# Turning two blocks of a cached page per instruction, and reordering the recurrence beside it

## The reference

```python
s_past = (einsum('blhr,bpr->bhlp', q_abs, ckv_past) + einsum('blhd,bpd->bhlp', q_pe, kpe_past)) * ATTN_SCALE
p      = softmax(concat([s_past, s_new]))
o_lat  = einsum('bhlp,bpr->blhr', p[..., :P], ckv_past) + einsum('bhlm,bmr->blhr', p[..., P:], ckv)
```

```python
sa = einsum('bhvk,bhk->bhv', S, kk_t)
S  = S * d_t[:, :, None, :] - sa[..., None] * b_t[:, :, None, :] + v_t[..., None] * k_t[:, :, None, :]
o  = einsum('bhvk,bhk->bhv', S, r_t)
```

## Time and profile before

| | |
|---|---|
| median of three runs | 2040.96 us |
| the profiled execution | 2037.07 us |
| its span, first to last instruction | 2035.4 us |
| TensorE busy (matmuls) | 1865.2 us, 92% |
| weight loads busy | 1164.3 us, 57% |
| VectorE busy | 895.6 us, 44% |
| ScalarE busy | 494.7 us, 24% |
| granted TensorE clock, mean | 0.970 |

### The profile page before, as it was taken

One profiled execution on the slowest core, in us unless ns is written; L12 is line 12 of the kernel. 1 busy time (PEld: TensorE's weight loads), 2 busy tenths in 40 slices (PEclk: granted clock), 3 DMA queues, 4 the chain that ended last, 5 costly groups with the idle time before them and its releaser, 6 DMA issues. The chain is left out here.

```text
span 2035.4 us, 45818 instructions
## 1 busy us (share of the span) xinstructions
PE 1865.2 (92%) x19360; PEld 1164.3 (57%) x19360; DVE 895.6 (44%) x1984; ACT 494.7 (24%) x1164; POOL 172.6 (8%) x158
## 2 busy tenths in 40 slices
PE   4899999999987999899949999999999879998898
PEld 2565676666654666654326656766666546665543
DVE  2024134222766676654230340332318577775542
ACT  3111012222412333311131110222224123333201
POOL 0010000011334000000000100000212240000000
PEclk9899999999999999979989999999999899999899
DMA  9500000000205666341075001010001166562411
GB/s 388 207 11 27 21 21 32 21 21 13 59 26 159 185 188 180 109 178 42 32 301 213 0 27 32 11 32 22 21 22 50 28 186 186 176 186 83 178 42 42
DMA packets 103927, 191.18 MB, mean 94 GB/s; under 512 B 17162, under 2 KB 87260, under 8 KB 100004
## 3 DMA queue, kind: packets, MB, share of 16 engines
q1 hardware_dynamic: 103716, 188.19, 27.9%
HBM read 175.41 MB, written 21.19 MB: 97 GB/s over the span
## 5 line engine op out<-in xcount | busy, mean ns | idle before, releaser
L771 PE MATMUL PB<-RB,R 128*128 128x344 f32 x1632 | 496.1, 457 | 0.0
L771 PEld LDWEIGHTS PB<-RB,R 128*128 128x128 f32 x1632 | 303.7, 191 | 159.6 <-issue 19.7
L1946 PE MATMUL PB<-RB,R 128*128 128x512 f32 x512 | 221.2, 593 | 0.0
L1589 PE MATMUL PB<-WUQ,Q 32*32 32x256 f32 x5120 | 191.0, 385 | 14.7 <-DVE WUQ L1748 9.4
L1748 DVE STREAM_TRANSPOSE WUQ<-RB 128x512 f32<-128x512 f32 x316 | 197.0, 676 | 5.5 <-DMA RB<-in_cache 5.3
L1946 PEld LDWEIGHTS PB<-RB,R 128*128 128x128 f32 x512 | 97.0, 190 | 120.8 <-issue 118.6
L931 ACT ACTIVATE R<-PB 128x344 f32<-128x344 f32 x90 | 41.2, 457 | 423.4 <-PE PB L771 423.4
L1184 DVE TENSOR_TENSOR PB<-PB,CST 128x128 f32<-128x128 f32 x64 | 18.8, 294 | 226.3 <-PE PB L791 226.3
L1589 PEld LDWEIGHTS PB<-WUQ,Q 32*32 32x32 f32 x5120 | 90.0, 104 | 46.0 <-DVE WUQ L1748 23.1
L619 PE MATMUL PB<-RB,R 128*128 128x344 f32 x288 | 88.5, 472 | 10.8 <-PEq L225 10.8
L619 PEld LDWEIGHTS PB<-RB,R 128*128 128x128 f32 x288 | 57.1, 199 | 41.4 <-issue 14.8
(11 more groups left out here) (355 smaller groups left out, 2619.6 us busy)
## 6 DMA issues: line engine op xcount, KB each, us to landing
RB<-in_cache SPq DMA_DIRECT2D x512, 160.0 KB, 2.6
R<-in_w_ada SPq DMA_DIRECT2D x16, 1536.0 KB, 17.4
R<-in_w_in SPq DMA_DIRECT2D x44, 512.0 KB, 3.7
RB<-in_w_out SPq DMA_DIRECT2D x8, 1024.0 KB, 9.9
RB<-out_x_stream SPq DMA_DIRECT2D x2, 4096.0 KB
out_x_stream<-RB SPq DMA_DIRECT2D x16, 512.0 KB
RB<-in_x_prompt SPq DMA_DIRECT2D x1, 4096.0 KB
RB<-in_w_kv SPq DMA_DIRECT2D x2, 1280.0 KB, 5.6
```

The costliest lines, as they stand in the source:

```text
L771: mm = pe.matmul(jobbank(j)[:, 0:CH], ring[:, blkno[n] % 4, k, :], hT[:, k, chunk(c)], start=(k == 0), stop=(k == KT - 1))
L1589: mm = pe.matmul(PB[qp[o], 2 * (h % 2) + q % 2, 0:256], Q4[qp[q], g, :], k[qp[q], c], start=(g == 0), stop=(g == NB - 1), skip_group_check ...
L1946: mm = pe.matmul(PB[0:n, 2 * (t % 2) + hf, :], mixT[:, k, cols(t)], wo[:, k, hf * 512:(hf + 1) * 512], start=(k == 0), stop=(k == 5))
```

## The change

Three edits. (1) A turn takes two blocks, 64 of the 320 columns, in one instruction of 128 x 1024 elements, into two neighbouring slots. kt_done and kt_used count pairs. At the place of an even S VectorE turns the next pair; TensorE waits before an even S and counts after an odd one. The turn in the stage before is merged likewise. (2) TA goes to bank 4, which it shares with PT, and waits for the copy of the probabilities of the even half instead of AK; PT of an odd half and Z wait for TA's copies; TB waits for AK. In STEPS Y5 and TB change places, so that an odd half ends with Y5, MX, TB, EX. (3) EX comes last in a half; an even half ends with Y2, MX, U1, X3, EX.

```diff
--- before.py
+++ after.py
@@ -1320,9 +1320,8 @@
                             dve.wait_ge(pg_in[0], 128)
                             dve.wait_ge(pg_in[1], 128)
                             pages = RB[:, HB[0]:HB[0] + 2 * QW].rearrange("p (s c) -> p s c", c=KW)
-                            for rb in range(2):
-                                dve.transpose(WUQ[:, rb * 512:(rb + 1) * 512].rearrange("p (j c) -> p j c", j=16),
-                                              pages[:, :, RP + 32 * rb:RP + 32 * rb + 32]).then_inc(kt_done, 1)
+                            dve.transpose(WUQ[:, 0:1024].rearrange("p (n j c) -> p j n c", n=2, j=16),
+                                          pages[:, :, RP:RP + 64].rearrange("p j (n c) -> p j n c", n=2)).then_inc(kt_done, 1)
 
 
             s_gs = sem("s_gs")
@@ -1402,7 +1401,7 @@
             fcol = lambda rb: RP + 32 * rb if rb < 8 else 32 * (rb - 8)
 
             STEPS = ["MA", "Z0", "X1", "U0", "Y1", "H0", "X2", "Z1", "Y2", "U1", "X3", "H1", "Y3", "OO",
-                     "X4", "AK", "Y4", "TA", "X5", "TB", "Y5"]
+                     "X4", "AK", "Y4", "TA", "X5", "Y5", "TB"]
             chain = ("Z", "U", "H", "O")
 
 
@@ -1418,7 +1417,7 @@
                     if rb < 8:
                         plan += [(h // 2, *mine.pop(0)), (h // 2, *mine.pop(0))]
                 rest = [(h // 2, *x) for x in mine]
-                plan += rest[:1] + [(h, "MX", 0)] + rest[1:2] + [(h, "EX", 0)] + rest[2:]
+                plan += rest[:1] + [(h, "MX", 0)] + rest[1:] + [(h, "EX", 0)]
             plan += [(NH - 1, "PT", 0), (NS, "rw", "Z0"), (NH - 1, "PV", 0), (0, "FC", 1), (NS, "rw", "U0"), (0, "FC", 2), (NS, "rw", "H0"),
                      (0, "FC", 3), (NS, "rw", "Z1"), (0, "FC", 4), (NS, "rw", "U1"), (0, "FC", 5), (NS, "rw", "H1"), (0, "FC", 6),
                      (NS, "rw", "OO")]
@@ -1475,14 +1474,14 @@
                                                start=True, stop=True, skip_group_check=True)
                             mm.then_inc(ak_full, 1)
                         elif n == "TA":
-                            pe.wait_ge(ak_done, p + 1)
+                            pe.wait_ge(pp_done, 2 * p + 1)
                             for f in range(2):
-                                pe.transpose(PB[:, 6, f * P:(f + 1) * P], A2[:, f, p * P:(p + 1) * P], ident)
+                                pe.transpose(PB[:, 4, f * P:(f + 1) * P], A2[:, f, p * P:(p + 1) * P], ident)
                             for f in range(2):
-                                mm = pe.transpose(PB[:, 6, (2 + f) * P:(3 + f) * P], pT[:, 2 + f, p * P + 1:(p + 1) * P + 1], ident)
+                                mm = pe.transpose(PB[:, 4, (2 + f) * P:(3 + f) * P], pT[:, 2 + f, p * P + 1:(p + 1) * P + 1], ident)
                             mm.then_inc(ta_full, 1)
                         elif n == "TB":
-                            pe.wait_ge(ta_done, p + 1)
+                            pe.wait_ge(ak_done, p + 1)
                             for f in range(2):
                                 mm = pe.transpose(PB[:, 6, f * P:(f + 1) * P], pT[:, 4 + f, p * P + 1:(p + 1) * P + 1], ident)
                             mm.then_inc(tb_full, 1)
@@ -1531,6 +1530,7 @@
                         i = 2 * p + c
                         bt, kt, vt = TOK[k][:, 0], TOK[k][:, 1], TOK[k][:, 2]
                         if n[0] == "Z":
+                            pe.wait_ge(ta_done, p + 1)
                             pe.wait_ge(tb_done, p + 1)
                             pe.wait_ge(st_done, i + 1)
                             for f in range(2):
@@ -1581,19 +1581,23 @@
                                 pe.wait_ge(sv_done, 1)
                             if g == 0 and h >= 2:
                                 pe.wait_ge(xe_done, h - 1)
-                            pe.wait_ge(kt_done, NB * h + g + 1)
+                            if g % 2 == 0:
+                                pe.wait_ge(kt_done, 5 * h + g // 2 + 1)
                             k = KTr[:, (NB * h + g) % 4].rearrange("p (s c) t -> p c s t", c=2)
                             for c in range(2):
                                 for q in (0, 2, 1, 3):
                                     o = 2 * (q // 2) + c
                                     mm = pe.matmul(PB[qp[o], 2 * (h % 2) + q % 2, 0:256], Q4[qp[q], g, :], k[qp[q], c], start=(g == 0), stop=(g == NB - 1),
                                                    skip_group_check=True, tile_position=(32 * q, 32 * o))
-                            mm.then_inc(kt_used, 1)
+                            if g % 2 == 1:
+                                mm.then_inc(kt_used, 1)
                         elif what == "PT":
 
                             pe.wait_ge(xe_done, h + 1)
                             if h:
                                 pe.wait_ge(pp_done, h)
+                            if h % 2 == 1:
+                                pe.wait_ge(ta_done, h // 2 + 1)
                             for s in range(4):
                                 mm = pe.transpose(PB[:, 4, s * P:(s + 1) * P], prb[:, s * P:(s + 1) * P], ident)
                             mm.then_inc(pp_full, 1)
@@ -1643,7 +1647,7 @@
                             op.then_inc(lo_done, 1)
                         elif n == "TA":
                             act.wait_ge(ta_full, p + 1)
-                            t6 = PB[:, 6, :].rearrange("p (v f w k) -> p v f w k", v=2, f=2, w=2)
+                            t6 = PB[:, 4, :].rearrange("p (v f w k) -> p v f w k", v=2, f=2, w=2)
                             for c in range(2):
                                 for w in range(2):
                                     op = act.activation(TOK[k][hp[w], 0:2, 2 * c:2 * c + 2, :], t6[hp[c], :, :, w, :], ACT.Identity)
@@ -1737,16 +1741,17 @@
                 @block.vector
                 def _(dve):
 
-                    def turn(n):
-                        h, rb = n // NB, n % NB
-                        if n >= 4:
-                            dve.wait_ge(kt_used, n - 3)
+                    def turn(i):
+                        h, rb = i // 5, 2 * (i % 5)
+                        if i >= 2:
+                            dve.wait_ge(kt_used, i - 1)
                         if rb == 0:
                             for q in (2 * h, 2 * h + 1):
                                 dve.wait_ge(pg_in[q % QS], 128 * (q // QS + 1))
                         pages = RB[:, HB[h % 3]:HB[h % 3] + 2 * QW].rearrange("p (s c) -> p s c", c=KW)
-                        op = dve.transpose(KTr[:, n % 4], pages[:, :, fcol(rb):fcol(rb) + 32])
-                        op.then_inc(kt_done, 1)
+                        o = 2 * (i % 2)
+                        dve.transpose(KTr[:, o:o + 2].rearrange("p n j c -> p j n c"),
+                                      pages[:, :, fcol(rb):fcol(rb) + 64].rearrange("p j (n c) -> p j n c", n=2)).then_inc(kt_done, 1)
 
                     dve.memset(S0[:, 0], 0.0)
                     dve.memset(Sg, 0.0)
@@ -1801,10 +1806,10 @@
                         elif what == "rw":
                             prepare(h, g)
                         elif what == "S":
-                            if NB * h + g + 2 < NB * NH:
-                                turn(NB * h + g + 2)
+                            if g % 2 == 0 and 5 * h + g // 2 + 1 < 5 * NH:
+                                turn(5 * h + g // 2 + 1)
                         elif what == "MX":
-                            dve.wait_ge(kt_used, NB * (h + 1))
+                            dve.wait_ge(kt_used, 5 * (h + 1))
                             dve.tensor_reduce(mxa, sc_(h), AX.XY, ALU.max)
                             dve.drain()
                             dve.tensor_copy(mxb[0:64], mxa[64:128])
```

## The result

The changed kernel took 2049.26 us (median of 6, 2042.84 to 2051.64), the kernel before on the same chips 2042.26 (6 runs, 2038.87 to 2044.92): ratio 1.0036 [1.002, 1.0051], slower by about 7.4 us. The forecast was +7.4, with a range of 2036 to 2056.

The account below looks back on a forecast made before the run. Neither engine is full; the wait that ends last at each place of a token's cycle bounds the kernel. 0.41 us over 16 cycles, plus 0.8 at the ends, gave +7.4 us, median 2048.4, range 2036 to 2056.

Parts of the forecast that it names:

- D: Length of one merged turn of two blocks on VectorE: 1.15 us, against 1.27 for a pair of single turns.
- Step 1: S4 and S5, even half: both blocks come at the merged turn's end, so PV starts 0.32 us later.
- Step 2: S8 and S9, even half: S8 0.49 us later; Y2 behind S9, the maxima and next turn also 0.49 later.
- rival B: Losses and gains cancel because VectorE keeps its saving from two pairs: 0 to +2 us, 2042, chance 0.26.
- Step 3: S2 and S3, odd half: S2 waits for the merged turn and starts 0.37 us later.
- the exponential's move: Exponential after X3's copy, freeing Y3: counted as nothing, hidden by the merged turn; about 0.4 us a cycle without the merge.
- Step 4: S8 and S9, odd half: nothing lost, since what follows waits for ScalarE in any case.
- TA, TB and Y5: Bank edit and new order at the odd half's end: +0.04 us a cycle, bounds -0.2 to +0.28.
- Sum: The cycle's loss of 0.41 us, 6.6 us over 16 cycles, plus 0.8 at the ends: +7.4 us.
- the end of a layer: Last PT of the decode stage waits for the exponential behind TB's copies: 0.4 us a layer, 0.8 in all.
- A: VectorE sets the pace and shorter turns pay: -5.8 us over 16 cycles, +0.8 at the ends, 2036, chance 0.21.
- C: The merged turn runs below the single one's rate or as two: near 1.34 us, total 2057, chance 0.09.

Follow-up runs that it names:

- n1: The kernel before with page loads from the seventh group of 8 pages on cut to one partition: 2033.42 us, 0.995.
- n3: The kernel before with the exponential last in a half and the later page loads cut to one partition: 2028.81 us, 0.9928.
- n2: The changed kernel with the later page loads cut to one partition: 2041.02 us, 0.9989 against the kernel before with full loads.
- e1: The kernel before with the merged turn alone; banks, order of steps and exponentials as before: 2050.26 us, 1.0032.
- e5: The kernel before with single turns, but TensorE starts a pair of blocks only when both are turned: 2050.42 us, 1.0038.
- e11: The changed kernel with blocks 4, 5 and 8, 9 of even halves turned and released singly again: 2038.9 us, 0.9993 against the kernel before.
- e8: The kernel before with block 4 of the even half turned ahead of MA's VectorE work: 2038.42 us, 0.9984.
- e2: The kernel before with only the exponential moved last in a half: 2041.45 us, 0.9994.
- e9: The kernel before with TA in bank 4, Y5 before TB, and X5's copy ahead of TA's on ScalarE: 2036.56 us, 0.9983.
- e10: The kernel before with the edits of e2, e8 and e9, plus blocks 8 and 9 of odd halves turned ahead of AK: 2035.93 us, 0.9973.

## Why the prediction was right

**D, the merged turn.** Forecast 1.15, measured 1.203. The straight line through 128 and 512 columns was too flat: 512 columns more cost 1.203 - 0.669 = 0.53 us, not 0.48. By the prediction's own steps that is 0.15 a cycle more, 2.4 us, and a forecast of +9.8. The estimate from "VectorE: DVE Perf Modes" of the Trainium skill (Specifications, 0.96 GHz), 1.20, was the right one; the trace agrees.

**Step 1 (S4 and S5, even half).** Forecast PV 0.32 late, measured 0.37 in the clean cycles and in after; with D = 1.20 the same step gives 0.37. One wait of 0.90, none at S5.

**Step 2 (S8 and S9, even half).** Forecast 0.49 for X3's side of the cycle; measured 0.60 at X3, and D = 1.20 accounts for it: the turn starts 0.05 later and lasts 0.05 longer. That VectorE then waits for Y2 (0.42 at 730.08) is what the step claimed against rival B.

**Step 3 (S2 and S3, odd half).** Forecast 0.37 at S2, with the exponential's move hidden; with D = 1.20 the same step gives 0.52, and 0.52 was measured, with a wait of 0.33 for the turn. The sum then carried this on to PT as it stood, and that was wrong: from S2 to PT it is 1.11 in the earlier trace rows and in n1, and 1.03 behind a wait, so 0.08 came back and PT is 0.44 late. That the exponential's move is worth 0.4 a cycle alone holds for a cycle without stops (n3: 0.5 in its shortest). Of the 6 to 7 us it brought 4.6 where the page loads are cut and 1.2 with them, at most 3.7 by the interval. The figure described the cycle, not the kernel.

**Step 4.** No loss at S8 and S9 of the odd half: the two MA differ by less (0.29) than the two PT (0.44).

**TA, TB and Y5.** The mis-sized term. Forecast +0.04, bounds -0.2 to +0.28; from PT to MA the clean cycles give 0.29 - 0.44 = -0.15. The order was as said (Y5 waits 0.76 for X5's copy, then TB, then S0), but Y5 came 2.60 after TA (743.67 less 741.07) in place of the 2.66 that I kept, and MA 1.78 after Y5 (745.45 less 743.67) in place of my 1.91: the change of tile shape that I counted between Y5 and TB, 0.17, is mostly not there.

**Sum.** 0.29 a cycle, 16 cycles: 4.6 us; at the end of a layer PT of n2 is 30.40 behind the last MA where n1's is 29.82, which is 0.58, of which 0.3 lies beyond the cycle's own: 0.6 in all, where I had 0.8. Together 5.2. The stages as a whole bear this out only when the stops of the last section are set aside: from the first MA to the last PT of both layers n2 takes 3.8 us more than n1 (476.1, 472.4), and 5.2 more with the mid-run stops taken off. Not every cycle is a clean one; the first two of a layer, for one, are together 0.4 to 0.7 shorter in n2. The rest of the 6.7 by which n2's profiled span is longer (2039.4, 2032.7) lies outside the stages, most of it in the stretch between them, where almost all of the code is the same; that stretch varies from 772.1 to 776.1 us over the 14 traces, so a single trace can't tell 2 us there.

So the forecast of +7.4 met the ratio partly by luck. The turn's true length would have made it 9.8; the 0.08 between S2 and PT, the order of Y5 (-0.15 where I had +0.04) and the end of the stage took about 4.5 of that back. The mechanism and the places are those forecast; 2 us between the steps' 5.2 and the measured 7.4 (7.6 in n2) stay open.

**The rivals.** A (VectorE sets the pace): fell with e1 and e5. The rule behind it, of the Trainium skill ("VectorE: DVE Perf Modes", on the fixed extra latency), that one large tile pays the latency once, agrees with VectorE's rows by about 0.07 us a pair (1.27 against 1.20), and the saving bought nothing where TensorE waited. B (they cancel): VectorE does wait for Y2, so its savings don't reach S2. C (D near 1.34): D is 1.203.

## What to carry to other kernels

Before two producer instructions are merged, look at who waits for the first one: the merge saves a fixed part (here about 0.07 us) and delays the first half by the whole second (here 0.53), and this costs wherever the consumer is that close. Leaving the two awaited pairs single took the loss away (e11: 1.0036 went to 0.9993); merging the pairs that were ready early did no harm and brought no gain that could be told. Moving the awaited turn ahead of other work did bring something (e8, 0.9984). And a wait that was taken off a cycle is not yet time: measure the edit alone, and if the gain is missing look for gaps without a releaser. A sum that comes out right is no proof of its terms: here four were off and three of them offset the first.

## What the runs showed of the hardware

TensorE's instructions themselves ran late. In the midst of 32 alike weight loads, with no wait written between them, the stream stops. The place is S0 and S1 of an odd half, in before (a whole row in 0.83, no stop) and in e2 (19 loads, a stop, 13 loads); weight loads of before, then of e2:

```profile
728.62 0.83 PEld L1589 LDWEIGHTS PB<-WUQ,Q 32*32 32x32 f32 x32
```

```profile
729.67 0.57 PEld L1589 LDWEIGHTS PB<-WUQ,Q 32*32 32x32 f32 x19
730.57 0.17 PEld L1589 LDWEIGHTS PB<-WUQ,Q 32*32 32x32 f32 x13 [0.33 <-issue]
731.15 0.20 PEld L1556 LDWEIGHTS PB<-R 64*64 64x64 f32 x4 [0.41 <-issue]
...
731.76 0.34 PEld L1522 LDWEIGHTS PB<-RB 32*32 32x32 f32 x32
```

The last row is Y3, which no longer waits for ScalarE: the stop took 0.33 of what that saved. In after the stop at the same place is 0.51 (732.14, shown above). Such stops lie 127 or 128 weight loads apart or multiples of that (in after behind the 1224th and 1352nd load of the first layer's stage, the 4658th and 4786th). With a matmul for each load that is about 256 instructions. The page of before, part 3, has a queue of instruction packets:

```profile
q8 instruction: 154, 2.52, 0.5%
```

2.52 MB in 154 packets is 16 KB a packet; if they were all TensorE's 38,720 instructions it would be 65 bytes each, so a packet would hold about 250. I read the stops as TensorE waiting for its next packet.

The kept traces have the start and the length of each packet of q8, and they settle that much. In the decode stages of all 14 traces there are 241 stops longer than 0.26 us between two weight loads of one line without a releaser. Every one of them ends 1.21 to 1.63 us after the end of a packet of q8, while these packets come 4.1 to 4.5 us apart in the median, and only about one weight load in ten of before's first stage lies in that stretch behind a packet. The packet took a median of 1.06 and 0.96 us in before's two stages.

Both layers' stages, from the first MA to the last PT, and these stops (gaps of 0.26 or less, most of them at PV and alike in every kernel, are not counted), in us:

| | stages | stops | stages less stops |
|---|---|---|---|
| before | 476.2 | 7.2 | 469.0 |
| after | 486.6 | 8.2 | 478.4 |
| e2 | 482.2 | 14.0 | 468.2 |
| e8 | 479.3 | 16.8 | 462.5 |
| e9 | 478.7 | 15.7 | 463.0 |
| e10 | 475.2 | 23.4 | 451.8 |
| n1 | 472.4 | 2.1 | 470.3 |
| n2 | 476.1 | 0.6 | 475.5 |
| n3 | 469.6 | 6.3 | 463.3 |

Where the kernel was made quicker the stops grew. With them set aside e10's stages are 17 us shorter than before's (24 were expected by the steps), e8's and e9's 6 (9 and 8), and n3's 7 shorter than n1's (5 to 7); only e2's, 1 us, stay far from their 6 to 7. The profiled execution of before was itself 4 to 5 us under the medians of its kernel, so these differences are low if anything. That is where most of e10's missing gain went, as far as single traces can tell. With the page loads cut the stops shrink from 7.2 to 2.1, which is 5 of the 10.2 us by which n1 is quicker.

What stays open: why the page loads make the stops longer, since the packets themselves took no less time without them (1.12 and 1.15 us in n1); why a quicker cycle stops more; and stops between unlike instructions, which are not in this count and may be in the 9.4 us by which after's last column exceeds before's.
